# Experts of a mixture in pairs: the products and the weight granules of two experts in turn

## The reference, cut to what matters

```
logits = tok @ w_router + b_router            # 256 tokens, 8 experts
top_p, top_i = top_k(softmax(logits), 2)      # every token goes to 2 experts
out = 0
for e in range(8):                            # D_FF = 3584
    gate, up = split(tok @ w_gate_up[e])      # 1024 x 7168
    out += gates[:, e] * ((silu(gate) * up) @ w_down[e])   # 3584 x 1024
```

## Time and profile before

| what | value |
|---|---|
| median of 3 runs | 1675.25 us (1674.47 to 1675.71) |
| profiled execution, its own time | 1677.06 us |
| its span | 1675.3 us |
| PE busy | 1467.0 us, 88% |
| PE weight loads | 1032.4 us, 62% |
| DVE busy | 652.9 us, 39% |
| ACT busy | 508.5 us, 30% |
| read from HBM | 471.47 MB, 282 GB/s over the span |
| mean granted TensorE clock | 0.941 of full speed |

### The profile page before, as it was taken

The page is one execution under the profiler, slowest core; times in us unless marked ns, Lnnn a source line. Parts: engine busy times, 40 slices in busy tenths (PEclk is TensorE's granted clock), DMA queues, the critical chain, the costliest instruction groups (busy, mean ns, idle before and its releaser), DMA issues.

```text
span 1675.3 us, 26810 instructions
## 1 busy us (share of the span) xinstructions
PE 1467.0 (88%) x11414; PEld 1032.4 (62%) x11415; DVE 652.9 (39%) x733; ACT 508.5 (30%) x622; POOL 33.9 (2%) x66
## 2 busy tenths in 40 slices
PE   3999999999997889999758999966999966978887
PEld 2763788886865467777535777753577744434443
DVE  5833444444007256665103666500567400101003
ACT  2332533342105144555003555300455301001001
POOL 2001000000000010000000000000000000000000
PEclk9979999999999989999977999997999988999898
DMA  8686865545841165777799877789999699999992
GB/s 289 255 301 237 312 254 201 189 165 196 303 151 51 52 250 201 270 283 252 282 393 393 301 282 263 250 317 396 391 393 388 231 389 394 391 395 392 380 393 105
DMA packets 206808, 474.63 MB, mean 283 GB/s; under 512 B 9987, under 2 KB 10031, under 8 KB 206671
## 3 DMA queue, kind: packets, MB, share of 16 engines
q1 hardware_dynamic: 199968, 470.83, 76.5%
q10 hardware_dynamic: 6702, 1.71, 0.5%
HBM read 471.47 MB, written 1.05 MB: 282 GB/s over the span
## 4 chain that ended last, share of the span: by engine, by line
PE 68%; SPq 16%; DMA 8%; issue 3%; DVE 2%; ACT 2%; ACTq 1%; POOL 0%; DVEq 0%
PE ps L1797 34%; SPq L394 16%; DMA ring<-in_moe_w_down_dram 5%; PE ps L1989 3%; PE ps L1880 3%; PE ps L2134 3%; PE ps L2043 3%; DMA ring<-in_ada_w_dram 3%; PE ps L2100 2%; PE ps L1969 2%; PE ps L1773 2%; PE ps L1977 2%; PE ps L1944 2%; PE ps L1888 2%; PE ps L2148 2%
## 5 line engine op out<-in xcount | busy, mean ns | idle before, releaser
L1510 DVE TENSOR_TENSOR ring_lo<-ring,w 128x2048 fp32r<-128x2048 f32 x119 | 272.5, 2292 | 142.9 <-ACT w L892 123.2
L892 ACT ACTIVATE w<-ring 128x2048 fp32r<-128x2048 f32 x119 | 227.7, 1915 | 188.8 <-PE ps L1797 173.1
L2043 PE MATMUL ps<-ring,arena 128*32 128x128 f32 (+1 forms) x3584 | 214.0, 342 | 74.6 <-DMA ring<-in_moe_w_gate_up_dram 67.1
L2043 PEld LDWEIGHTS ps<-ring,arena 128*32 128x32 f32 (+1 forms) x3584 | 157.9, 134 | 137.8 <-issue 73.2
L1797 PE MATMUL ps<-ring_lo,x_hi 128*128 128x512 f32 x532 | 208.0, 391 | 0.0
L1485 DVE TENSOR_TENSOR arena<-arena,ps 128x128 f32<-128x128 f32 (+1 forms) x35 | 11.9, 341 | 375.6 <-PE ps L2043 375.6
L2100 PE MATMUL ps<-ring,arena 128*32 128x512 f32 (+1 forms) x560 | 106.5, 692 | 33.5 <-DMA ring<-in_moe_w_down_dram 33.5
L855 ACT ACTIVATE arena<-ps 128x128 f32<-128x128 f32 (+1 forms) x35 | 11.2, 320 | 404.8 <-PE ps L2043 404.8
L1201 DVE TENSOR_TENSOR ring_lo<-ring,w_hi 128x2048 fp32r<-128x2048 f32 x42 | 95.6, 2290 | 88.0 <-ACT w_hi L646 88.0
L1797 PE MATMUL ps<-w,x_hi 128*128 128x512 f32 x308 | 127.0, 412 | 0.1
L1797 PE MATMUL ps<-w,x_lo 128*128 128x512 f32 x308 | 120.5, 391 | 0.0
(11 more groups left out here) (349 smaller groups left out, 1867.8 us busy)
## 6 DMA issues: line engine op xcount, KB each, us to landing
ring<-in_moe_w_gate_up_dram SPq DMA_DIRECT2D x112, 2048.0 KB, 18.2
ring<-in_moe_w_down_dram SPq DMA_DIRECT2D x56, 2048.0 KB, 18.6
ring<-in_ada_w_dram SPq DMA_DIRECT2D x24, 2048.0 KB, 11.3
ring<-in_ffn_w_gate_up_dram SPq DMA_DIRECT2D x14, 2048.0 KB, 12.9
ring<-in_ffn_w_down_dram SPq DMA_DIRECT2D x7, 2048.0 KB, 8.2
ring<-in_sb_w_qkv_dram SPq DMA_DIRECT2D x6, 2048.0 KB, 9.0
ring<-in_s_w_out_dram SPq DMA_DIRECT2D x2, 2048.0 KB, 7.9
ring<-in_sb_w_out_dram SPq DMA_DIRECT2D x2, 2048.0 KB, 15.6
```

Source lines behind the costliest of these rows:

```text
L892: act.activation(half3(h).bitcast(F32R), ff_half(gran(N_MOE + g), half), ACT.Copy).then_inc(whi_done, 2 if g in plain else 1)
L1510: dve.tensor_tensor(ff_half(ring_lo[(N_MOE + g) % RING][:, :], half).bitcast(F32R), ff_half(gran(N_MOE + g), half), half3(h), ALU.subtract ...
L2043: ins = pe.matmul(ps[width * r:width * r + width, bank, 0:cols], x[:, k, 0:width], weights[:, k, cols * r:cols * r + cols], start=k == 0, ...
```

## The change

Where the largest expert has at most 160 tokens and at least four of experts 1 to 7 are light (at most 64 tokens), the eight turns become four turns of two experts. A new table puts in places 0 to 3 the first of each pair (expert 0, then the other wide ones, then light ones that are left) and in places 4 to 7 the second of each pair, always light. Otherwise the old loop runs, which is kept in an Else branch (only indented, not shown).

In a pair, SP loads the granules of the first (`a`) and of the second (`b`) in the order of `pair_order`; the second's step f-1 goes beside the first's step f, its down product beside f+1:

```diff
+def pair_order():
+
+    order = [("ag", 0), ("au", 0), ("ag", 1), ("au", 1), ("ad", 0), ("bg", 0), ("ad", 1), ("bu", 0), ("ag", 2)]
+    for f in range(2, FB):
+        order += [("au", f), ("bg", f - 1), ("ad", f), ("bu", f - 1)]
+        if f < FB - 1:
+            order += [("ag", f + 1)]
+        order += [("bd", f - 2)]
+    return order + [("bg", FB - 1), ("bu", FB - 1), ("bd", FB - 2), ("bd", FB - 1)]
+AHEAD = 5
```

Before the routing is known, SP loads only the first five granules (`AHEAD`, all of expert 0), and the others behind `route_done`; before, it could load all 21 of expert 0. PE's body of a pair with a wide first expert (`tail` is true for 129 to 160 tokens), and the end of a pair:

```diff
+                tail_in("ag", 0, TAIL_GATE, t_gate)
+                gather_second(p)
+                for f in range(FB):
+                    tail_in("au", f, TAIL_UP, t_up)
+                    main_gate(f)
+                    tail_turn(f)
+                    if f:
+                        second_in(p, "bg", f - 1, width)
+                    else:
+                        pair_weights(p)
+                    tail_down(f)
+                    main_up(f)
+                    if f:
+                        second_in(p, "bu", f - 1, width)
+                    main_turn(f)
+                    tail_in("ag", f + 1, TAIL_GATE, t_gate)
+                    if f > 1:
+                        second_down(p, f - 2, width)
+                    main_down(f)
+                    if f:
+                        second_turn(p, f - 1, width)
+                pair_end(p, width)
+            def pair_end(p, width):
+
+                second_in(p, "bg", FB - 1, width)
+                gather(p + 1)
+                second_in(p, "bu", FB - 1, width)
+                second_down(p, FB - 2, width)
+                second_turn(p, FB - 1, width)
+                second_down(p, FB - 1, width)
```

```diff
+            def scatter_pair(p):
+
+                pe.wait_ge(ysb_act, p + 2)
+                pe.wait_ge(ysb_dve, p + 2)
+                for i in range(4):
+                    tt, h = divmod(i, 2)
+                    rows_h = slice(64 * h, 64 * h + 64)
+                    tokens_t = slice(P * tt, P * tt + P)
+                    pe.matmul(ps[:, Y_BANK + i, :], scT[:, 0, tokens_t], ysb4[:, h, :], start=True, stop=False)
+                    pe.matmul(ps[:, Y_BANK + i, :], scT[rows_h, 1, tokens_t], ysb4[rows_h, 2, :], start=False, stop=False)
+                    pe.matmul(ps[:, Y_BANK + i, :], scT2[rows_h, tokens_t], ysb4[rows_h, 3, :], start=False, stop=True
+                              ).then_inc(sc_ps, 1)
```

DVE at the start of a wide pair:

```diff
+                w_rest(0)
+                product_tail(0)
+                w_rest(1)
+                second_out(p)
+                weigh_pair(p, ((0, slots[:, 2, :]),), width)
+                for f in range(FB):
+                    n = 3 * f
+                    if f:
+                        product_tail(f)
+                    w_rest(2 * n + 2)
+                    if f == 0:
+                        for i in range(4):
+                            add_scattered(p + PAIRS, i)
+                    w_rest(2 * n + 3)
+                    if f == 0:
+                        keep_pair_weights(p)
```

1338 lines of the change are left out of this document (906 added, 432 removed).

## The result

| | median | lowest to highest |
|---|---|---|
| before | 1674.86 us | 1671.26 to 1675.71, 4 runs |
| after | 1625.47 us | 1619.09 to 1634.89, 4 runs |

The ratio is 0.9714 (95% interval 0.9663 to 0.9765): 49 us less, where 107 less were forecast, and 1625 lies above the range of 1548 to 1612. The profiled execution of the change took 1627.29 us, its span 1625.5.

What follows compares the result with a forecast made beforehand. It took PE as the bound in two of eight turns, the loads in the others, and the loads in pairs. Granule 10's start 676 + 842 for 158 granules + 18 pauses + 2 restart + 30 end = 1568 us; range 1548 to 1612.

Steps and rivals of the forecast that it cites:

- granule 10 starts at: Start of the first pair: granule 10's load waits for the second expert-step's up slot and starts at 676 us.
- from the last landing to the end: End of the kernel: 31.9 us now, about 6 saved by the earlier gather, 3.6 added by four scatter matmuls: 30.
- the bound and the step: Wide pairs: loads set the pace at 32.0 us a step; PE needs 29.5 with a tail and waits 2 to 3.
- PE or the handshake becomes the bound: Rival for the wide pairs: steps of 33.5 to 35 us instead of 32; 1602 us, range 1588 to 1630; chance 26%.
- the ring starves: Rival: slots come back late, loads in pairs 0 and 1 fall to 262 GB/s, 224 us more, 1792 us; chance 6%.
- The pauses between the pairs: Loads pause at pair starts for want of slots: 13 us for pair 1, 5 for pair 2, 0 for pair 3.
- some 2.5 of branches: Between pairs: PE's branches take 2.5 us of the 16 from a pair's last landing to the next pair's start.
- The last granule of a pair lands at L; PE takes 2 us for it: End of a pair: 2 us of PE work behind the last landing, then copy, scatter and branches; next pair at L+16.
- The releases of the second gate and up: Start of a tail pair: these slots come free 41 and 50.5 us after it, at L+57 and L+66.5.
- a start from rest costs another 2: Loads after a pause: a lone transfer takes 7.9 us, so restarting adds 2 us, counted once in the sum.
- signs for its own failure: Pair starts: the forecast would be wrong there if the dips in load rate were much longer than 13 us.
- faster loads: Rival: loads exceed 394 GB/s, pairs fall to PE's 4.92 us a granule, 777 us instead of 842, total 1503; chance 4%.

Runs made afterwards that it cites:

- after_ring32: The changed kernel with eight more numbers in turn_i, so its ring begins at byte 39200, not 39168; 1656.5 us, ratio 0.9895.
- straight: The changed kernel with the loop over pairs and choice of bodies written out on PE, DVE and ACT for these inputs' kinds; 1585.1 us, ratio 0.9474.
- before_straight2: The kernel before with its eight expert bodies written out in a row, in the experts' turn, on PE, DVE and ACT; 1660.3 us, ratio 0.9900.
- straight_narrow: The changed kernel written out without jumps, with pair 2's second expert back at width 32 instead of 64; 1573.9 us, ratio 0.9390.
- hold_loads: The changed kernel with SP holding pair 0's loads from granule 5 on until PE's first product of that pair; 1617.4 us, ratio 0.9689.
- branch_order: The changed kernel with a pair's four bodies in the other order, tail with width 32 first and light last; 1638.3 us, ratio 0.9796.

## Why the prediction was wrong

It worked with 5.33 us a granule, so its sum is best held against after_ring32, the change at that rate. All are spans; granule 10's start and the last landing (1619.0, 1587.7, 1550.5) are read from the queue's issues and their landings.

| term | forecast | after_ring32 | after | straight |
|---|---|---|---|---|
| granule 10 starts at | 676 | 695 | 690 | 682 |
| 158 granules | 842 | 842 | 804 | 804 |
| holes and what else the loads lost | 20 | 82 | 94 | 64 |
| from the last landing to the end | 30 | 37 | 38 | 37 |
| sum | 1568 | 1656 | 1626 | 1587 |

**Right: the bound and the step.** Pairs with a tail run at the rate of the loads. A step takes PE 28.80 us, 29.5 forecast, and PE waits 2.31 us for the second expert's down granule where "about 2 to 3" stood. The rival that PE or the handshake becomes the bound fell, although 1625 lies inside its 1588 to 1630: the stretches at 408 to 412 GB/s leave no room for a step of 33.5 to 35. So did "the ring starves". Four more switches of the tiling mode, weighed at 31.5 us a step, didn't show: 28.80 holds all of them. The Trainium skill, TensorEngine Tiling (Array Packing), section Key Properties, says that such a switch drains the TensorE; the trace shows no cost of it beyond what the products' own durations hold.

**Wrong: the pauses.** The pauses between the pairs, put at 18 us (13 for pair 1, 5 for pair 2 and 0 for pair 3), are the step that failed; at the prediction's own rate it was 74 in the three holes of after_ring32 (30, 18 and 26), 82 with all that the loads lost. Four parts of it:
- *"some 2.5 of branches"*, and of issue waits "nothing to 10 here as most is hidden". By straight, jumps cost 40 us. In the profiled executions it is 38: 7 in the start of pair 0 (689.5 against 682.1), 30 in what the loads lose behind it (94 against 64, of it 26 in the three holes, 85 against 59), and 1 behind the last landing. They were read from a kernel whose loop body is shorter and whose stalls are small (7.4 us), and before_straight2 shows that 15 us lay there already. The fall of the clock in one scatter, 9 us, goes with it: it follows PE's short stall at 1361 and is not there in straight, where that scatter takes 11.8.
- *"The last granule of a pair lands at L; PE takes 2 us for it"*. From the last granule for which PE waits, the down granule ahead of au(6), nine more of 5.33 land until L, 48.0 us. In that time PE has, by the prediction's own rows, eight products of the second expert, four main granules, two of the tail, a gather of 7.3 and the turns. That is some 50.5 us in width 32, so L + 2.5, and the prediction's 2 was near for pairs 0 and 1. Pair 2 has no tail but width 64: 61.1 us, L + 13.1. After_ring32 has 4.8, 4.7 and 16.5, with products at the low clock and PE's short waits for ACT that are not in the count. The prediction knew that pair 2 runs in width 64, and still counted "with shorter work" and no hole behind it. At 5.09 a granule the same counts give L + 4.7 and L + 15.3; straight has 4.9, 6.5 and 17.2, and straight_narrow 4.3 with the hole gone.
- *The releases of the second gate and up, 41 and 50.5 behind a start.* By the queue of straight they come at 43.7 and 53.1 in pair 1. The prediction took 3 us off its 44 and 53.5 because that start runs at the full clock. But it is DVE that sets the pace there, as it says itself: PE waits 3.3 us for DVE's additions.
- *"a start from rest costs another 2"*, once. Each hole ends with one: granule 10 of pair 1 takes 9.0 us from issue to landing in straight, 3.9 over the 5.09 of a granule in the row.

With these, in straight: pair 0's last granule lands at L = 849.4 and PE starts pair 1 at 867.0, or L + 17.7 where L + 16 stood. Granule 10 goes at 920.1, or L + 70.8 (66.5 forecast), where its turn was L + 50.9. That is 19.9 and 3.9 for the start from rest, and the hole is 23 us by its rate. The way of counting was right, its inputs weren't; faster loads make the hole longer by themselves, since the chain that ends it is PE's.

The start of pair 0 and the end were smaller misses. Of the 6 us that granule 10 is late in straight, 3.4 are the second gather, which ran at the low clock (7.09 us, 3.7 forecast). At the end the gather did move ahead of the last landing, but three products of width 64 stand behind it, so that PE ends 12.6 us behind that landing, where it took 13.0 in before: next to nothing of the 6 us was saved.

The prediction's signs for its own failure held: three dips and not two, each much longer than 13 us, and starts 248, 245 and 257 us apart in place of 224 to 237.

**Half right: "faster loads", 4%.** The prediction held 394 GB/s to be the ceiling and set aside the 425 that it cites from the Trainium skill, HBM Reference, opening section. 412 was there to be had, but by a shift of 32 bytes that the diff brings along unasked. The rival's 1503, from PE's 4.92 us a granule, was wrong: at 5.09 the loads still set the pace. The shift gave 38 us of transfer time and took some of that back in the holes: 31 us by after_ring32.

**How the 49 us come about.** Moving the ring gives 24 (1675.4 to 1651.4), the pairs on top of it 26 (to 1625.5). So half of the gain is luck, as nobody meant to move the ring. Of the 52 that pairs are worth without jumps, the new jumps take half. What the forecast called the gain of the change, 107 us, is 19 when the ring lies 32 bytes behind a multiple of 256 (after_ring32, 1656.5 against 1675.4), and 23 at 64 bytes behind one (1651.5 against 1674.7).

**What stays open.** What a single jump costs, as a function of its distance and of the DMA queue's state, wasn't measured by itself. That the falling clock follows from the stall is read from traces and no run was made for it: the scatter in front of pair 3 behaves so in after, after_ring32 and hold_loads (stalls of 2.65, 3.03 and 2.66 us), three scatters of branch_order do too (4.48, 4.25 and 2.72), and none of straight does, where PE waits at most 0.90 us ahead of one.

## What to carry to other kernels

A loop whose body is one of several long pieces of code can pay for its far jumps on each engine, here 40 us of 1625, most of it in the pauses of the loads between two bodies: put the likely case in a row behind a test at the top, and leave the loop for the rest. When a change adds or resizes any buffer, look where the targets of the large loads begin now; a rate that moves by a few per cent at a full DMA share is a sign of it, and a comparison should be made with both kernels on the same alignment. At a hand-over between two stages, count all the work that stands behind the last wait against the loads that still come, for each kind of stage with its own widths, instead of taking the last landing as the end. And a queue that waits for slots says nothing about the bound as long as the loads ahead of it run at full rate.

## What the runs showed of the hardware

- Loads of 2 MB with rows of 2 or 4 KB into SBUF ran at 411 to 412 GB/s, in stretches without a pause, where the ring begins at a multiple of 256 bytes and at 393 to 394 where it begins 32, 64 or 224 bytes behind one. The Trainium skill, DMA: Bandwidth & Descriptors, section How a descriptor splits into AXI transactions, says that transactions start at multiples of 256 B, and that a descriptor which doesn't start at one begins with a transaction from the boundary below it; it tells this of reads. By an estimate from that page a 2 KB piece takes 9 transactions instead of 8; the measured loss, 4.6%, is less than that ratio, and equal for starts 32, 64 and 224 behind a multiple.
- At the first entry to a body behind two far branches PE, DVE and ACT stood still for 16.8, 15.4 and 11.9 us. With that body first behind the branch DVE stood 3.1. With no weights in flight PE stood 11.3.
- A stall of PE of 2.65 us was followed by 21.2 us of scatter, most of it at a granted clock of 0.50 and 2.08 us for a product that takes 1.10 at 1.00. It cost 9 us, more than three times its length.
